# Storing the combine stage's weights as high and low parts in a scratch tensor during the branch stage

## What is computed

```python
q, k, v, z_a, u_b, z_b, g_a, g_b = split(h @ w_in)      # h: (2048 + 8, 1024)
a = combine_groups(attention outputs, lse)              # (L, 512)
p = pool_mix(u_b, ...)                                  # (L, 512)
ya = (a * silu(z_a)) @ w_a_out                          # w_a_out: (512, 1024)
yb = (p * silu(z_b)) @ w_b_out                          # w_b_out: (512, 1024)
m = sigmoid(g_a) * ya + sigmoid(g_b) * yb
y = x + gate * (m @ w_out)                              # w_out: (1024, 1024)
```

## Time and profile before

| | |
|---|---|
| median of 3 runs | 2242.29 us (2240.03 to 2243.05) |
| the profiled execution | 2242.48 us; its span, first to last instruction, 2240.7 us |
| TensorE busy | 2168.6 us, 97% of the span |
| VectorE, ScalarE, GpSimd busy | 836.4, 592.5, 241.2 us (37%, 26%, 11%) |
| mean granted clock of TensorE | 0.987 of 2.4 GHz |
| branch stage ends, combine stage begins | about 1826 and 1830 us of the span |
| first matmul of the combine stage's first feature tile | 1841.25 us |
| transposes of the second half of chunk 1, 2 | 1898.08, 1944.12 us |

### The profile page before, as it was taken

One profiled execution on the slowest core, in us unless ns is written; L12 is line 12 of the kernel. 1 busy time (PEld: TensorE's weight loads), 2 busy tenths in 40 slices (PEclk: granted clock), 3 DMA queues, 4 the chain that ended last, 5 costly groups with the idle time before them and its releaser, 6 DMA issues. The chain is left out here.

```text
span 2240.7 us, 36856 instructions
## 1 busy us (share of the span) xinstructions
PE 2168.6 (97%) x12795; PEld 2041.4 (91%) x12795; DVE 836.4 (37%) x2257; ACT 592.5 (26%) x2152; POOL 241.2 (11%) x378
## 2 busy tenths in 40 slices
PE   7799999999999999999989999999999978999999
PEld 2499999999999999999979899999999976998897
DVE  3623333333333333333331343121222327666563
ACT  3523333333333333333331111111111122111010
POOL 1122121111111111111100000000000002000000
PEclk9899999999999999999999999999999989999999
DMA  9357657655646545455251333555323245544441
GB/s 336 114 174 237 202 189 222 203 175 175 197 148 192 178 157 175 160 167 163 84 170 76 117 128 132 159 158 170 101 97 115 94 139 213 171 162 142 142 132 50
DMA packets 252177, 354.04 MB, mean 158 GB/s; under 512 B 19597, under 2 KB 225685, under 8 KB 250615
## 3 DMA queue, kind: packets, MB, share of 16 engines
q1 hardware_dynamic: 207577, 309.82, 42.6%
q10 hardware_dynamic: 44454, 42.33, 5.7%
HBM read 256.52 MB, written 183.77 MB: 196 GB/s over the span
## 5 line engine op out<-in xcount | busy, mean ns | idle before, releaser
L984 PE MATMUL a_pp<-a_wH,hH 128*128 128x384 f32 x1536 | 532.6, 347 | 11.8 <-DVE a_wL L1261 11.8
L986 PE MATMUL a_pp<-a_wH,hL 128*128 128x384 f32 x1536 | 521.1, 339 | 0.0
L985 PE MATMUL a_pp<-a_wL,hH 128*128 128x384 f32 x1536 | 519.4, 338 | 0.0
L984 PE MATMUL pp<-hH,wH 128*128 128x412 f32 (+1 forms) x1120 | 393.7, 351 | 6.0 <-DVE wL L674 6.0
L985 PE MATMUL pp<-hL,wH 128*128 128x412 f32 (+1 forms) x1120 | 392.2, 350 | 0.0
L986 PE MATMUL pp<-hH,wL 128*128 128x412 f32 (+1 forms) x1120 | 391.9, 350 | 0.0
L984 PEld LDWEIGHTS a_pp<-a_wH,hH 128*128 128x128 f32 x1536 | 289.8, 189 | 12.1 <-DVE a_wL L1261 12.1
L985 PEld LDWEIGHTS a_pp<-a_wL,hH 128*128 128x128 f32 x1536 | 290.0, 189 | 0.0
L986 PEld LDWEIGHTS a_pp<-a_wH,hL 128*128 128x128 f32 x1536 | 289.0, 188 | 0.0
L1213 ACT ACTIVATE a_junk<-a_pp 128x128 f32<-128x128 f32 x384 | 106.5, 277 | 582.9 <-PE a_pp L986 576.8
L1272 DVE TENSOR_SCALAR a_ms<-a_ss 128x2 f32<-128x2 f32 (+1 forms) x204 | 34.4, 169 | 599.1 <-ACT a_junk L1213 599.1
(11 more groups left out here) (208 smaller groups left out, 2968.4 us busy)
## 6 DMA issues: line engine op xcount, KB each, us to landing
out_dram<-in_state_kv_w_dram SPq DMA_DIRECT2D x64, 1023.5 KB, 6.1
qkv_dram<-qkv SPq DMA_DIRECT2D x192, 192.0 KB, 2.0
qkv_in<-qkv_dram SPq DMA_DIRECT2D x192, 192.0 KB, 2.6
w_first<-in_w_in_dram SPq DMA_DIRECT2D x46, 512.0 KB, 6.7
gl<-gT_dram SPq DMA_DIRECT2D x64, 264.0 KB
gT_dram<-ost ACTq DMA_DIRECT2D x80, 206.0 KB, 2.5
out_dram<-in_state_kv_w_dram SPq DMA_DIRECT2D x8, 2044.0 KB, 10.8
o_dram<-ot ACTq DMA_DIRECT2D x192, 65.0 KB, 2.2
```

The costliest lines, as they stand in the source:

```text
L984: nc.tensor.matmul(out, sH, mH, start=(i == 0), stop=False)
L985: nc.tensor.matmul(out, sH, mL, start=False, stop=False)
L986: last = nc.tensor.matmul(out, sL, mH, start=False, stop=(i == len(terms) - 1))
```

## The change

The splitting of the combine stage's weights moves into the branch stage. Beside each of its last sixteen tiles (12 to 27) the kernel loads one tile of 128 columns of the weights (1024 rows: m = 0 to 7 of `w_a_out` over `w_b_out`, m = 8 to 15 of `w_out`) into `x_st`; GpSimd makes the high part `xH`, VectorE the low part `xL` (in the place of `x_st`), and SP stores both to two scratch tensors `wc_dram`, in the layout that the combine stage holds in SBUF. These tiles share their place in SBUF with `gst`, `pst` and `sp_rows`, which are no longer in use then; SP waits for that. The two value iterations and the last loads of SP are written out.

In the combine stage `w_whole` and all its splits go. SP loads both parts straight into `m_wH` and `m_wL`: 4 pieces for the branch weights (all 8 row tiles of a quarter of the columns) and 4 for `w_out`, each as two DMAs of 1024 KB, and TensorE waits for the loads. The order at the start becomes: `zl`, `bl`, piece 0, gates 0 and 1, piece 1, gates 2 and 3, pieces 2 to 4, gates 4 and 5, pieces 5 to 7, gates 6 and 7, and on as before.

```diff
+    wc_dram = [nc.dram_tensor(f"wc_dram{i}", [P, 2 * KT, D], F32, kind="Internal").ap() for i in range(2)]
...
+with ExitStack() as later:
+    xH = scope(later)[0]("xH", [P, KT, P], F32R)
+    with ExitStack() as same_place:
+        x_st = scope(same_place)[0]("x_st", [P, KT, P])
+    xL = scope(later)[0]("xL", [P, KT, P], F32R)
...
+        def load_combine(m, col, last=False):
+
+            sp.wait_ge(x_stored, m * 32 + LEAD_DMA)
+            for i, w in enumerate((v["w_a_out"][0], v["w_b_out"][0])):
+                if last:
+                    w = v["w_out"][0][i * D // 2:(i + 1) * D // 2, :]
+                apart(sp, v["passed"])
+                sp.dma_start(x_st[:, 4 * i:4 * i + 4, :], w.rearrange("(k p) c -> p k c", p=P)[:, :, bass.ds(col, P)]).then_inc(x_landed, 16)
+
+        def store_combine(m, col, last=False):
+
+            sp.wait_ge(x_lo, after(m))
+            for part, dram in zip((xH, xL), v["wc_dram"]):
+                sp.dma_start(dram[:, KT * last:KT * last + KT, bass.ds(col, P)], part[:, :, :].bitcast(F32)).then_inc(x_stored, 16)
...
+        sp.wait_ge(spT_done, 1)
+        for i in range(2):
+            sp.wait_ge(b_stored[i], 16 * PAIRS * NBC // 2)
         with sp.Fori(0, NS // 2) as i:
             n = i * 2 + SCORE0
             for j in range(2):
                 load(n + j, j, gate_column(n + j))
+                load_combine(i * 2 + j, (i * 2 + j) * P)
                 keys(i * 2 + j)
                 shifted_copy(sp, v, 0, i * 2 + j, bulk)
+                store_combine(i * 2 + j, (i * 2 + j) * P)
         load(SOFT0, 0, gate_column(SOFT0))
+        load_combine(KT, 0, True)
         load(SOFT0 + 1, 1, gate_column(SOFT0 + 1))
+        store_combine(KT, 0, True)
+        load_combine(KT + 1, P, True)
         sp.wait_ge(out_stored[NBC - 1], LEAD_DMA + 16 * 4)
         sp.dma_start(zs[:, :, :], gT_dram[0:4, :, SEQ:TT].rearrange("f p t -> p f t")).then_inc(zs_in, 16)
         sp.wait_ge(p_ready, 2)
         sp.dma_start(pnew_dram.rearrange("b h g -> (b h) g"), pcn[:, :]).then_inc(pn_out, 16)
         sp.wait_ge(pn_out, 16)
         sp.dma_start(pn[:, :], pnew_dram.rearrange("b h g -> b (h g)")).then_inc(pn_in, 16)
-        with sp.Fori(0, 2) as i:
-            n = i * 2 + VALUE0
+        store_combine(KT + 1, P, True)
+        for n in range(4):
+            load(VALUE0 + n, n % 2, gate_column(VALUE0 + n))
+            m = KT + 2 + n
+            load_combine(m, (m - KT) * P, True)
             for j in range(2):
-                load(n + j, j, gate_column(n + j))
-            for j in range(4):
-                values(i * 4 + j, j % 2)
-        load(END0, 0, gate_column(END0))
-        load(END0 + 1, 1, gate_column(END0 + 1))
+                values(2 * n + j, j)
+            store_combine(m, (m - KT) * P, True)
+        for n in range(2):
+            load(END0 + n, n, gate_column(END0 + n))
+            m = KT + 6 + n
+            load_combine(m, (m - KT) * P, True)
+            store_combine(m, (m - KT) * P, True)
         sp.wait_ge(late, 48)
-        for i in range(2):
-            sp.wait_ge(b_stored[i], 16 * PAIRS * NBC // 2)
+        sp.wait_ge(x_stored, 2 * KT * 32 + LEAD_DMA)
 
     @block.gpsimd
     def _(pool):
...
-        with pool.Fori(1, NF // 2) as i:
+        with pool.Fori(1, SCORE0 // 2) as i:
             split_hi(i * 2, 0, i * 16 + 16)
             split_hi(i * 2 + 1, 1, i * 16 + 16)
+        with pool.Fori(SCORE0 // 2, NF // 2) as i:
+            for j in range(2):
+                split_hi(i * 2 + j, j, i * 16 + 16)
+                pool.wait_ge(x_landed, (i * 2 + j) * 32 + (32 - SCORE0 * 32))
+                apart(pool, v["passed"])
+                nc.gpsimd.tensor_copy(xH[:, :, :], x_st[:, :, :]).then_inc(x_hi, 1)
 
     @block.vector
     def _(dve):
...
+
+        def combine_lo(m):
+
+            dve.wait_ge(x_hi, m + 1)
+            nc.vector.tensor_tensor(xL[:, :, :], x_st[:, :, :], xH[:, :, :].bitcast(F32), ALU.subtract).then_inc(x_lo, 1)
 
         def split_lo(n, slot):
...
+                combine_lo(i * 2 + j)
                 score(i * 2 + j)
 
-        split_lo(SOFT0, 0)
-        split_lo(SOFT0 + 1, 1)
+        for n in range(2):
+            split_lo(SOFT0 + n, n)
+            combine_lo(KT + n)
         dve.wait_ge(scT_done, 1)
         chained(nc.vector.tensor_copy(scr[:, :], ppool[0][0:BH, 0:GROUPS * P]))
...
-
-HI_AT = {1: (4,), 2: (5,), 3: (6, 7, 8), 4: (9,), 6: (10,), 7: (11,)}
-LO_AT = {1: (4,), 2: (5,), 3: (6, 7), 7: (10,), 8: (11,)}
-
-
 GROUPS_AT = ({KT - 1: 0}, {3: 0, KT - 1: 1}, {})
-POOLED = (8, 9)
...
-                w, k0 = (w_a, 0) if tiles.start < 4 else (w_b, 4) if tiles.start < KT else (w_o, KT)
-                sp.dma_start(w_whole[:, tiles, cols], w[(tiles.start - k0) * P:(tiles.stop - k0) * P, cols]
-                             .rearrange("(k p) c -> p k c", p=P)).then_inc(wo_landed[n], 16)
+                for part, dram in zip((wH, wL), v["wc_dram"]):
+                    sp.dma_start(part[:, tiles, cols].bitcast(F32), dram[:, tiles, cols]).then_inc(wo_landed[n], 16)
 
         for i in range(NT):
             sp.sem_inc(ol_in[i], 16)
         branch_inputs(0)
-        load_weights(range(4))
+        load_weights(range(1))
         gates(0, range(0, 2))
+        load_weights(range(1, 2))
         gates(0, range(2, RG))
-        load_weights(range(4, 10))
+        load_weights(range(2, 5))
         gates(0, range(4, 6))
-        load_weights(range(10, len(pieces)))
+        load_weights(range(5, len(pieces)))
         gates(0, range(6, KT))
         sp.dma_start(gate_b[:, :], gate_dram[0:1, :].to_broadcast([P, D])).then_inc(gate_in, 16)
 
...
 
-        for i, n in enumerate(POOLED):
-            tiles, cols = pieces[n]
-            pool.wait_ge(w_whole_hi, n + 1)
-            nc.gpsimd.tensor_tensor(wL[:, tiles, cols], w_whole[:, tiles, cols], wH[:, tiles, cols].bitcast(F32),
-                                    ALU.subtract).then_inc(w_pool_split, 1)
-
         def body(c, last):
...
             def before(k):
                 pe.wait_ge(m_lo, after(c * KT + k))
-                if k % 2 == 0 and k < 2 * len(POOLED):
-                    pe.wait_ge(w_pool_split, k // 2 + 1)
-                elif k % 2 == 0:
-                    pe.wait_ge(w_split, KT + k // 2 - len(POOLED) + 1)
+                if k % 2 == 0:
+                    pe.wait_ge(wo_landed[4 + k // 2], 32)
             return before
...
             for f in range(KT):
                 if f % 2 == 0:
-                    pe.wait_ge(w_split, f + 2)
+                    pe.wait_ge(wo_landed[f // 2], 32)
                 branch(c, f, last)
```

## The result

The changed kernel takes **2248.64 us** (median of 8 runs, 2247.1 to 2249.6) against 2241.16 us of the kernel before (8 runs, 2240.03 to 2243.05): a ratio of 1.0032 with a 95% interval of 1.0021 to 1.0043, so it is slower by 7.5 us. The profiled execution took 2248.93 us (span 2247.1), 0.3 above its median.

A forecast was written before the change was run, and what follows sets the result against it. TensorE (97% busy) was held in the combine stage's first chunk by 15.5 us of split waits, with the DMA full too. Profiled 2242.5 + 7.0 (first chunk) + 0 (branch stage) = 2249.5 us; range 2241.5 to 2257.

The forecast's parts named there:

- group sums: First chunk of combine stage, VectorE: the first waits for `ol` at 1891.7 us and takes 4.6 us, ending at 1896.3.
- second result ends: First chunk, TensorE: 24 matmuls end at 1898.5 us with late clock return, or at 1896.5 with early return.
- second transposes: End of first chunk, the anchor: 1905.3 or 1904.5 us against 1898.08 before; +7.0 us taken.
- The landing times: Combine stage's DMA queue: 0.35 MB/us for 1 KB runs, 0.415 for pieces 4 to 7; gate 7 lands at 1885.9 us.
- The clock of TensorE: Second result of first chunk: full clock returns 8.8 us after 1887.1, making 13 matmuls slow, or after 4.2 us.
- The branch stage at nothing: Sixteen branch tiles: added loads, splits and stores hide under 22.2 us tiles; 0, between 0 and +1 us.
- the tile that I called the tightest: Branch stage, value tiles: the split before tile 26, its load behind two stores, has 5 us left.
- (1): Combine-stage queue runs at its best rate throughout, 0.43 MB/us: 2241.5 us, the same time; chance 0.20 with halfway cases.
- halfway case: Combine-stage queue with rates halfway to the best: +3 us, 2245.5; chance included in the best-rate rival's 0.20.
- (2): First chunk: the splits alone were the bound and the DMA has room; 15 us less, 2227.5 us; chance 0.05.
- (3): Combine-stage loads: scratch tensors read slower than inputs, 0.30 MB/us; 13 us more, 2262.5 us; chance 0.06.
- (4): Branch stage: a tile comes late behind the stores, +2 to +6 us beside the 7, 2254 us; chance 0.07.

The follow-up runs named there:

- h7: `h4` with piece 10 (third of the four `w_out` pieces) sent ahead of gates 6 and 7: 2230.89 us, 0.9953 of before.
- e3: The change with the loads of gates 6 and 7 sent ahead of weight pieces 6 and 7: 2248.94 us, 1.0034 of before.
- e1: Only the change's branch stage, splits and stores included; the combine stage is the one of before, loading whole weights: 2242.05 us, 0.9999 of before.
- e6: The change with branch weights laid out by quarters, runs of 8 KB instead of 1 KB, same bytes: 2245.31 us, 1.0014 of before.
- e2: The change without loading the weights' low parts; TensorE reads the high parts instead, with as many matmuls: 2226.20 us, 0.9934 of before.
- h6: The change, but all weights loaded whole and split by ScalarE and VectorE, last gates and `ol` loaded earlier: 2234.93 us, 0.9971 of before.
- h4: `h6` with the last two pieces of `w_out` loaded as stored parts instead of whole and split: 2231.77 us, 0.9955 of before.

## Why the prediction was right, step by step

The forecast was 2249.5 us, the median is 2248.64; against the profiled time of before the sum said +7.0, and the first chunk grew by 7.6, the medians differ by 7.5 us. Counted from the issue of `zl` (the prediction's times stand on before's clock, so 1829.53 is taken off):

| step | predicted | measured |
|---|---|---|
| first matmul | 12.1 | 12.0 |
| gated product for k = 6 (gate 6 lands) | 55.6 | 56.3 |
| group sums (first `ol` lands) | 62.2 | 62.6 |
| second result ends | 69.0 or 67.0 | 68.3 |
| second transposes | 75.8 or 75.0, 75.55 taken | 76.2 |

- **The landing times.** Right within 0.7 us over 62, with two rates: 0.35 MB/us for the 1 KB runs (351 and 362 GB/s measured) and 0.415 for the 8 KB runs (412 from 1866 to 1886). The Trainium skill ("DMA: Bandwidth & Descriptors", Specifications) has both a share of 358 GB/s and a ceiling of 435 GB/s; 412 GB/s over twenty microseconds, and 436 over three in `h7`, side with the ceiling.
- **The clock of TensorE.** I chose a return 8.8 us after the first matmul behind the gap, with 4.2 as the other end. It came after about 5.4 us (from 1886.81 to 1892.2: 0.50 up to 1892, 0.94 in the window from 1892 to 1894). It decided nothing: the second result ended at 1896.7 and VectorE was busy with the first until 1897.79. So the path that held is that of the early return, for which the sum gave 75.0.
- **The size.** From 75.0 to the 76.2 measured 1.2 us are missing: 0.5 is the later landing of `ol`, and 0.7 is a result operation of VectorE that took 1.40 us beside a GpSimd copy, which the sum had at 0.7. That the forecast of 75.55 is only 0.6 off is in part luck: it had taken some of the late return, which didn't come, and it had nothing for the copy, which did.
- **What sets the end.** This step was read half right. The chain from `ol` over both group sums to the transposes was in the sum, and it is what the chain that ended last shows:

```profile
1877.04 13.99 DMA ol<-o_dram
1892.54 1.77 DVE ol L1021
```

  But I gave as much room to the gates of k = 6 and 7 and the matmuls behind them. `e3` moved them by 10 us and the end stayed.
- **The branch stage at nothing.** Right, by `e1`. In the tile that I called the tightest the low part of the weights was ready 6.2 us ahead of tile 26, where 5 us were forecast. Timelines of SP, GpSimd and VectorE after:

```profile
1757.11 0.42 SPq L612 DMA_DIRECT2D wc_dram<-xH  x1
1757.58 1.06 SPq L612 DMA_DIRECT2D wc_dram<-xL  x1
1758.76 3.92 SPq L576 DMA_DIRECT2D w_first<-in_w_in_dram  x1
```

```profile
1768.58 1.04 POOL L695 CAST wH<-w_first 128x1024 fp32r<-128x1024 f32 x1 [22.46 <-DMA w_first<-in_w_in_dram]
```

```profile
1769.65 1.23 DVE L723 TENSOR_TENSOR wL<-w_first,wH 128x1024 fp32r<-128x1024 f32 x1 [4.21 <-POOL wH L695]
```

  The split began at 1765.47 before and begins at 1768.58 now, behind two stores, 3.1 us later by the clock and 4.2 against the stage, which lies 1.1 us earlier here; the low part is done at 1770.9, and tile 26 starts at 1777.1 (1778.19 less 1.1). The window of the middle of the stage shows the added work beside a TensorE that is as busy as before (columns as in the earlier trace rows):

```profile
1433.90:1478.90 45.00, 45.00 (x242) 44.89 (x242) 14.19 (x16) 6.59 (x12) 4.22 (x5) 1.00 0.77 234
```

- **The rivals.** (1), the best rate throughout, did not come: the short runs stayed at 351 to 362. Part of what it would have been worth is seen in `e6`, where the branch pieces come at 382 to 420: 3.3 us less, 2245.31, which is its halfway case (2245.5). (2) needs free bytes; with them its time is right (`e2`). (3) fell: 351 GB/s from scratch. (4) fell: no matmul of a tile waited for `wL`.
- **What bounded before.** I read the waits for splits as the bound and the full DMA as the second. `h6` shows a third thing: with the bytes of before and all splits on ScalarE and VectorE, 6.7 us go by order and placing alone. By its chain that ended last, in which no transfer stands behind `zl`, the full DMA did not hold before back. That the change trades the waits for splits for a full queue was right; that before's arrangement left 6.7 us on the table I did not see.

## What to carry to other kernels

Before work is moved away by storing its result, count the bytes that the result has more than its source and lay them on the queue of the stage that reads it: in a full queue 8.4 MB more cost more than the 15.5 us of waits that they removed, while the same parts taken only for the last pieces, for which there is both time to land and a split that would be late, gave a gain. Look at the order of the queue first: a transfer that waits for its buffer stops every transfer behind it (5.2 us of SP in `h4`), and the one to send early is the one that the last chain starts from, not the one with the longest wait in the list.

## What the runs showed of the hardware

**VectorE beside GpSimd.** In before, two VectorE operations on 256 columns with both operands in SBUF took 4.68 and 4.54 us where they take 0.42 otherwise, and each ran while GpSimd split a piece. VectorE and GpSimd in before:

```profile
1859.31 4.68 DVE L1652 TENSOR_TENSOR m<-gm 128x256 f32<-128x256 f32 x1
...
1866.59 4.54 DVE L1654 TENSOR_TENSOR mL<-m,mH 128x256 fp32r<-128x256 f32 x1 [0.62 <-ACT mH L1574]
```

```profile
1859.12 4.60 POOL L1542 TENSOR_TENSOR m_wL<-w_whole,m_wH 128x2048 fp32r<-128x2048 f32 x1 [79.89 <-ACT m_wH L1589]
...
1866.33 4.52 POOL L1542 TENSOR_TENSOR m_wL<-w_whole,m_wH 128x2048 fp32r<-128x2048 f32 x1 [2.62 <-ACT m_wH L1589]
```

The result operation of 1.40 us in the changed kernel (above; 0.69 otherwise) stands beside a GpSimd copy that began at 1896.18 and took 1.07 us. The Trainium skill ("SBUF — State Buffer", SBUF: two separate sides) has the two engines take one pair of ports as a lock that is held for the whole instruction; these three cases agree with that. VectorE does the same split in 2.28 us (in `h6`), so this split, given to GpSimd, cost VectorE more (4.68 - 0.42 = 4.3 us) than doing it. How much of the 6.7 us of `h6` comes from here is only estimated (above).

**Run length and rate.** One core's loads moved 351 GB/s in runs of 1 KB at a DMA share of 1.10, and 382 to 420 with the branch weights in runs of 8 KB at 1.00: with short runs the engines are as full, and less goes through.

**The clock.** Behind gaps, TensorE's clock came back from 0.50 (1.2 GHz) to 1.00 (2.4 GHz) at three distances: in before 4.2 us after the first matmul of the stage and 8.85 us after the first one behind the later gap, in the changed kernel some 5.4 us after the first one behind its last gap. One figure for it would have been wrong by up to twice.
